# One expert slot loaded in pieces, products that nothing reads, and a first output store in two parts

## The reference

```python
def reference(x, p, ...):
    x = first_block(x, p, ...)      # stick-breaking and latent attention, conv + gated FFN, gated embedding
    x = second_block(x, c_2, ...)   # modulated conv / sparse attention / pooling mixer, then the experts
    return x

# the end of the second block
h = _rmsnorm(x, norm2_g) * (1 + sc2) + sh2
x = x + g2 * _hier_moe(h, ...)      # 32 experts in 4 groups; each token takes one group and its best two
return _rmsnorm(x, final_g)

# one expert, over the tokens that chose it
(silu(hb @ w1[e]) * (hb @ w3[e])) @ w2[e]      # 1024 -> 512 -> 1024
```

## Time and profile before

| | us |
|---|---|
| three runs, median (lowest to highest) | 928.71 (927.51 to 929.39) |
| the profiled execution, its own time | 927.32 |
| its span in the profile | 925.3 |
| PE busy / PEld / DVE / ACT / POOL | 780.2 / 528.0 / 382.2 / 327.5 / 125.7 |
| read from HBM | 296.55 MB |

### The profile page before, as it was taken

The page is one execution under the profiler, slowest core; times in us unless marked ns, Lnnn a source line. Parts: engine busy times, 40 slices in busy tenths (PEclk is TensorE's granted clock), DMA queues, the critical chain, the costliest instruction groups (busy, mean ns, idle before and its releaser), DMA issues.

```text
span 925.3 us, 12760 instructions
## 1 busy us (share of the span) xinstructions
PE 780.2 (84%) x5334; PEld 528.0 (57%) x5334; DVE 382.2 (41%) x837; ACT 327.5 (35%) x652; POOL 125.7 (14%) x129
## 2 busy tenths in 40 slices
PE   9999999999999999999999997567675566656765
PEld 7986578999998877898786342123221222212214
DVE  6747865667779764899613110010100101001002
ACT  5656656666665466834723010001000000000012
POOL 0011031555541034102110000000000000000000
PEclk9999999999999999999999999789878988988877
DMA  9956708754069782655479999999999999999995
GB/s 353 419 192 233 306 1 356 268 184 183 35 246 397 300 316 94 251 183 201 164 290 421 431 426 428 429 429 425 428 428 427 429 427 428 429 426 429 428 425 239
DMA packets 24543, 298.48 MB, mean 323 GB/s; under 512 B 2720, under 2 KB 3104, under 8 KB 5920
## 3 DMA queue, kind: packets, MB, share of 16 engines
q1 hardware_dynamic: 24480, 297.61, 78.3%
HBM read 296.55 MB, written 1.05 MB: 322 GB/s over the span
## 4 chain that ended last, share of the span: by engine, by line
PE 61%; DMA 33%; ACT 3%; DVE 2%; issue 0%; DVEq 0%; ACTq 0%
PE ps L108 60%; DMA ring<-in_exps 33%; PE ps L111 1%; ACT fr L117 1%; ACT sq L114 1%; ACT ar L117 0%; ACT ar L114 0%; DVE xg L134 0%; DVE ar L126 0%; DVE misc L149 0%; DVE yT L126 0%; ACT L114 0%; DVE yT L130 0%; DVE sq L134 0%; ACT hT L114 0%
## 5 line engine op out<-in xcount | busy, mean ns | idle before, releaser
L108 PE MATMUL ps<-fr 128*128 128x256 f32 (+2 forms) x1308 | 208.0, 316 | 0.9 <-POOL fr L126 0.4
L108 PE MATMUL ps<-ring,sq 128*32 128x512 f32 x944 | 137.4, 717 | 75.5 <-DMA ring<-in_exps 75.1
L108 PEld LDWEIGHTS ps<-fr 128*128 128x128 f32 (+1 forms) x1308 | 184.4, 191 | 18.5 <-DVE fr L126 1.9
L108 PE MATMUL ps<-ring,ar 128*32 128x512 f32 (+4 forms) x792 | 97.4, 583 | 45.5 <-DMA ring<-in_exps 39.4
L108 PEld LDWEIGHTS ps<-ring,sq 128*32 128x32 f32 x944 | 28.8, 121 | 172.6 <-DMA ring<-in_exps 119.7
L126 DVE TENSOR_TENSOR fr<-ring,fr 128x512 fp32r<-128x512 f32 (+2 forms) x121 | 93.8, 803 | 44.2 <-ACT fr L117 43.9
L126 DVE TENSOR_TENSOR ar<-ar,ps 128x512 f32<-128x512 f32 x9 | 6.2, 687 | 250.9 <-PE ps L108 250.9
L117 ACT ACTIVATE fr<-ring 128x512 fp32r<-128x512 f32 (+1 forms) x139 | 80.0, 622 | 25.9 <-PE ps L108 23.1
L117 ACT ACTIVATE ar<-ps 128x512 f32<-128x512 f32 (+4 forms) x48 | 27.2, 571 | 166.0 <-PE ps L111 139.4
L108 PEld LDWEIGHTS ps<-ring,ar 128*32 128x32 f32 (+1 forms) x792 | 26.6, 120 | 100.3 <-DMA ring<-in_exps 58.5
L126 DVE TENSOR_TENSOR ar<-ps,ar 128x512 f32<-128x512 f32 (+6 forms) x38 | 23.4, 632 | 117.2 <-PE ps L108 116.9
(11 more groups left out here) (187 smaller groups left out, 908.7 us busy)
## 6 DMA issues: line engine op xcount, KB each, us to landing
ring<-in_exps SPq DMA_DIRECT2D x85, 2048.0 KB, 30.9
ring<-in_modw SPq DMA_DIRECT2D x12, 2048.0 KB, 12.7
ring<-in_wup SPq DMA_DIRECT2D x11, 2048.0 KB, 13.3
ring<-in_wdown SPq DMA_DIRECT2D x5, 2048.0 KB, 12.8
ar<-in_exps SPq DMA_DIRECT2D x5, 2048.0 KB, 12.9
ring<-in_win SPq DMA_DIRECT2D x4, 2048.0 KB, 11.2
ring<-in_exps SPq DMA_DIRECT2D x7, 1024.0 KB, 9.0
ring<-in_wo SPq DMA_DIRECT2D x2, 2048.0 KB, 8.8
```

The lines of the kernel that those rows point to most:

```text
L108: return Issue(self.e and self.e.matmul(o, l, r, start=start, stop=stop, skip_group_check=True))
```

## The change

It does four things. Slot 8 is described as three pieces of 2048, 1536 and 512 columns; the third holds the place of the mask. The first two are issued after slot 5, with waits for the mask and for the last sum of the pooling, ahead of slot 7; the third follows slot 7. Slot 17, which has the same place, is loaded in the same three pieces. Slot 14 of the ring is loaded in halves like 12 and 13. PE gets products that nothing reads: 8 in the first joint, and in the last group 16 before each slot from the third on, 4 before the transposes, 3 after them and 12 between the first two parts of the end; PE's wait for a root of the first block (`act_wo["root", 1]`) is passed some instructions earlier. The first output tile is scaled and stored in two parts, each with 256 columns of either half.

```diff
--- before.py
+++ after.py
@@ -421,6 +421,7 @@
                  sd.rearrange("p a t -> p (a t)"), ar[:, 3584:4096]]
         more = {3: [hT[:, :], ar[:, 1536:3584]], 6: spare}
         more.update({7 + i: [ar[:, 4096 + SLOT * i:4096 + SLOT * (i + 1)]] for i in range(3)})
+        more[8] = [ar[:, 8192:10240], ar[:, 10752:12288], ar[:, 10240:10752]]
         more.update({17: more[8], 18: more[9]})
         part8, whole = misc[:, 16:32], misc[:, 32:38]
         END = GROUPS - 1
@@ -445,7 +446,7 @@
         def expert_in(j):
             if j in more:
                 return landed[f"again{j}" if j > 11 else f"more{j}"]["all"]
-            return loaded("exps", j, int(j in (12, 13)))
+            return loaded("exps", j, int(j in (12, 13, 14)))
 
 
         END_PARTS = ((0, 256), (256, 256), (512, 128), (640, 128), (768, 128), (896, 64), (960, 64))
@@ -764,8 +765,12 @@
 
             pe.wait_ge(act_wo["o", 1])
             to_features("mix", (6, 7, 0, 1))
+            pe.wait_ge(act_wo["root", 1])
+            idle_products(2, 5)
             token_sums("mix", 2, dve_joint["mix", "mt", 1, 0])
+            idle_products(3, 5)
             token_columns("mix", 2)
+            idle_products(3, 5)
             pe.wait_ge(dve_joint["mix", "rrecip"])
             turned_over(3, misc[:, 118:120]).then_inc(pe_joint, "mix", "over")
             mod_total(1, act_wo["root", 1])
@@ -1133,6 +1138,8 @@
                             over_tokens(j - 2)
                         for kk in range(2):
                             k = 2 * s + kk
+                            if g == END and 4 * m + s > 1 and kk == 0:
+                                idle_products(16, 2)
                             pe.wait_ge(expert_in(j))
                             if m == 0:
                                 pe.wait_ge(*x_ready(g, k))
@@ -1148,6 +1155,8 @@
                     spread_row(0, mod[:, 40:48], ((act_exp["x", 0, 7], dve_exp["x", 0, 6]), ()))
                 elif g < END:
                     gather(g + 1, 0)
+                if g == END:
+                    idle_products(4, 3)
                 pe.wait_ge(dve_exp["av", g])
                 for k in range(4):
                     t = pe.transpose(ps[:, 0, 128 * k:128 * k + 128], ar[:, av + 128 * k:av + 128 * k + 128], ident)
@@ -1179,6 +1188,7 @@
                     spread_row(1, col("final_g", 0, 8), ((dve_exp["x", 3, 3],), (act_exp["x", 3, 7],)))
 
 
+            idle_products(3, 3)
             pe.wait_ge(act_exp["aT", END], dve_exp["st", END])
             def end_sum(i):
                 lo, n = END_PARTS[i]
@@ -1202,6 +1212,7 @@
                 t.then_inc(pe_end, "y", i)
 
             end_products(0)
+            idle_products(12, 3)
             end_products(1)
             end_sum(0)
             end_sum(1)
@@ -1686,8 +1697,10 @@
                 row_root(whole[:, 2 + j:3 + j], whole[:, j:j + 1], 1024).then_inc(act_end, "root", j)
             for j in range(2):
                 act.wait_ge(dve_end["recip", j], dve_end["gain", 1])
-                o = sq[:, 1024 * j:1024 * j + 512]
-                act.copy(o, o, whole[:, 4 + j:5 + j]).then_inc(act_end, "out", j)
+                for i in range(2 - j):
+                    n = 512 if j else 256
+                    o = sq[:, 1024 * j + n * i:1024 * j + n * i + n]
+                    act.copy(o, o, whole[:, 4 + j:5 + j]).then_inc(act_end, "out", j, i)
 
         def vector(dve):
             def rest(signal, name, k, ready):
@@ -2271,9 +2284,11 @@
                 dve.wait_ge(act_end["root", j])
                 t = dve.reciprocal(whole[:, 4 + j:5 + j], whole[:, 2 + j:3 + j]).then_inc(dve_end, "recip", j)
                 dve.wait_ge(t)
-                o = 1024 * j + 512
-                dve.scalar_tensor_tensor(sq[:, o:o + 512], bank(YB[2 * j + 1]), whole[:, 4 + j:5 + j], ar[:, FROW + 512:FROW + 1024],
-                                         ALU.mult, ALU.mult).then_inc(dve_end, "out", j)
+                for i in range(2 - j):
+                    n = 512 if j else 256
+                    o = 512 + n * i
+                    dve.scalar_tensor_tensor(sq[:, 1024 * j + o:1024 * j + o + n], bank(YB[2 * j + 1], n * i, n * i + n), whole[:, 4 + j:5 + j],
+                                             ar[:, FROW + o:FROW + o + n], ALU.mult, ALU.mult).then_inc(dve_end, "out", j, i)
 
         def gpsimd(pool):
 
@@ -2421,7 +2436,7 @@
             def ring_load(name, j):
                 n = {("win", 3): 3584, ("wqkv", 0): 3072, ("wdown", 5): 2048, ("wple", 0): 2048, ("win2", 3): 2048,
                      ("wsm2", 0): 3104}.get((name, j), SLOT)
-                if name == "exps" and j in (12, 13):
+                if name == "exps" and j in (12, 13, 14):
                     for h in range(2):
                         sp.wait_ge(*used(*BEFORE[name, j], h))
                         sp.dma_start(slot(name, j)[:, 2048 * h:2048 * h + 2048],
@@ -2438,12 +2453,13 @@
                     return
                 sp.dma_start(slot(name, j)[:, 0:n], A[name][j][:, 0:n]).then_inc(ring_in[PLACE[name, j]], name, j, 0)
 
-            def more_load(j, name, *free):
+            def more_load(j, name, *free, places=(0, 8)):
                 lo = 0
                 sp.wait_ge(*free)
-                for o in more[j]:
+                for i, o in enumerate(more[j]):
                     n = o.shape[1]
-                    sp.dma_start(o, A["exps"][j][:, lo:lo + n]).then_inc(landed[name], "all")
+                    if places[0] <= i < places[1]:
+                        sp.dma_start(o, A["exps"][j][:, lo:lo + n]).then_inc(landed[name], "all")
                     lo += n
 
             for name, j in STREAM[:-2]:
@@ -2460,9 +2476,11 @@
                 if (name, j) == ("exps", 4):
                     more_load(3, "more3", pe_conv["qu", 1], dve_in2["glu"])
                 elif (name, j) == ("exps", 5):
+                    more_load(8, "more8", dve_in2["mask"], pool_conv["pm"], places=(0, 2))
                     more_load(7, "more7", pe_out2["pool", 1], pe_out2["rbias"], pe_soft["dsa", "values", 3], act_out2["at", 0], act_out2["at", 1],
                               dve_conv["tap", 30, 1], pool_conv["pm"], pool_conv["rwg"], dve_out2["rbias"], act_out2["pool", 1])
-                    for i in (8, 9, 6):
+                    more_load(8, "more8", places=(2, 3))
+                    for i in (9, 6):
                         more_load(i, f"more{i}")
                 elif (name, j) == ("exps", 16):
                     for i in (17, 18):
@@ -2475,9 +2493,12 @@
                     sp.wait_ge(*used(*BEFORE["exps", j]))
                 o, lo = last_place(i), lo % SLOT
                 sp.dma_start(ring[:, o:o + n], A["exps"][j][:, lo:lo + n]).then_inc(landed[f"last{i - 2}"], "all")
-            for j in range(2):
-                sp.wait_ge(act_end["out", j], dve_end["out", j])
-                sp.dma_start(out[:, 1024 * j:1024 * j + 1024], sq[:, 1024 * j:1024 * j + 1024]).then_inc(stored, "out", j)
+            for i in range(2):
+                sp.wait_ge(act_end["out", 0, i], dve_end["out", 0, i])
+                o, x = (v[:, 0:1024].rearrange("p (h c) -> p h c", c=512)[:, :, 256 * i:256 * i + 256] for v in (out, sq))
+                sp.dma_start(o, x).then_inc(stored, "out", 0, i)
+            sp.wait_ge(act_end["out", 1, 0], dve_end["out", 1, 0])
+            sp.dma_start(out[:, 1024:2048], sq[:, 1024:2048]).then_inc(stored, "out", 1)
 
 
         gT, grow, gbc, oa, osl, kept = 1024, 1536, 2048, 2560, 4608, 7936
@@ -2647,7 +2668,7 @@
             p = Program(e)
             sync(p)
             when_flagged(p, over_sync)
-            e.wait_ge(stored.sem, 32)
+            e.wait_ge(stored.sem, stored.final)
 
         @block.tensor
         def _(e):
```

## The result

The changed kernel takes 930.18 us (median of 20 runs, 928.78 to 933.83) against 928.47 for the kernel before in the same comparison (20 runs, 927.15 to 930.04). The ratio is 1.0021, with a 95% interval of 1.0013 to 1.0029: 1.9 us slower (1.2 to 2.7). The ratio is worked out from all runs and is not that of the two medians. The forecast was 927.5, no change or a little faster. So the two profiles lie 4.7 us apart, more than the medians do, and part of that is chance.

The account below looks back on a forecast made before the run. Up to 468 us compute was taken to set the time, from there the loads still to come. Terms -1.3 - 1.5 + 1.8 - 0.2 = -1.2 us gave a median of 927.5 us, range 924.9 to 930.0.

Parts of the forecast that it names:

- A: First joint: eight products keep the clock up, so the FFN's 24 matmuls take 3.06 instead of 4.43 us; -1.3 us.
- the "yes" to whether the next weight tile is ready: FFN's start: the tile is ready at 150.1 us, before PE gets to it at 150.3 after 48 matmuls.
- B: Slot 8 in early pieces: 4.30 us leave the stream behind 468, a restart at slot 12 takes part back; -1.5 us.
- 1.65 us earlier than now, and all behind it by the same: Slot 12's first half lands at 502.35 us, 1.65 earlier, and all later loads keep that gain.
- The load of 468.0: 2 MB load that met an empty queue: 8.0 us to landing instead of 4.91, pricing a restart at 3.1 us.
- Rival 3: One upstream gain missing: slot 12's half still needs 7.2 us, or the joint's clock falls anyway; 929.0 us, chance 0.16.
- C: Last group: sixteen products make a slot cost PE 5.64 us while one lands every 4.91; +1.8 us.
- Rival 4: Last group's products run at the low clock, making the change slower: 931.0 us, chance 0.08.
- D: First output tile's store in parts: first store up to 0.4 us earlier, last up to 0.4 later; -0.2 us.
- The rivals with a gain (1 and 2): First: last group's products never delay PE, 925.7 us, chance 0.22; second: slot 12's restart costs less, 926.2 us, chance 0.10.

Follow-up runs that it names:

- the group alone: Kernel before with only the idle products of the last group added: 930.36 us, ratio 1.0024 (1.0014 to 1.0035).
- The parts alone: Kernel before with one part each: joint products and earlier wait, 0.9984; slots 8, 14, 17 in pieces or halves, 0.9995; last group's products, 1.0024.

## Why the prediction was wrong

- **A, -1.3, was right in size**: -1.5 measured (0.6 to 2.4), the joint 0.12 longer where 0.1 was taken, 24 matmuls in 3.10 where 3.06 was worked out. One step in it failed, the "yes" to whether the next weight tile is ready: PE waits for it and some 0.3 us are lost, 1.0 instead of 1.3 against the profile of before. That the measured gain is no smaller than forecast is luck: the other executions without the products mostly lose more than that profile (5.0 to 5.3 us for the 24 matmuls in three of five, 4.6 in one). That the kernel before loses this time in most executions, but not in all, one profile could not show.
- **B, -1.5, was wrong**, in the step "1.65 us earlier than now, and all behind it by the same". The first clause held: 5.1 us from issue to landing (5.55 forecast), 1.86 us earlier. By the Trainium skill, DMA: Bandwidth & Descriptors, section Anatomy of one DMA, it would have been 4.4 us, an estimate from what that page gives for loads issued by GpSimd; the 5.1 of this trace, for a load issued by SP, does not bear it out. The second clause failed at once. A restart was priced once, for one half; but slot 12's second half is also issued only when PE lets its place go, 2.1 us after the first. It meets a queue as thin and pays again: 4.30 us behind the first half instead of 2.45, which puts it where it was. The load of 468.0, from which the price was taken, did not show this: its successor stood in the queue 0.4 us later and landed 5.3 us behind it, near the 4.91 of the full stream. Rival 3 had B's gain missing (sum +0.3), but for slot 12's first half, the one that did gain.
- **C, +1.8, was too small.** The mechanism held in every number that the profile of before could give: 5.62 us a slot (5.64), 0.73 lost with each, no idle time, full clock; alone it cost 2.2 us (1.3 to 3.3), in the changed kernel 3.5. What was missed is how PE enters the group. The earlier trace rows begin with a group entered at full clock; in nine of the fourteen profiles the slot before it runs at the low clock and takes 2.9 to 3.6 us instead of 1.9. PE then comes to the third slot 1.8 us later against its landing (2.54 late in the changed kernel, 0.76 with the group alone), and as it has no idle time from there on, all of that reaches the end: 4.9 us of lag there against 2.4 (a late landing in the latter is the other 0.6). Without the products 2.8 us of idle time before the third slot absorb it. Whether the low clock there is chance or comes with the other parts stays open: eight of the nine profiles whose FFN starts at full clock have it, and one of the five others. Rival 4 looked for the low clock inside the group, where it never came.
- **D, -0.2**: nothing in the traces, and below what the runs can tell.
- **The sum**: the forecast's -1.2 lies 3.1 below the measured +1.9. With C as the changed kernel has it (3.5) it missed B by 1.5 and C by 1.7. That -1.5 and 0 and 3.5 and 0 come to the measured value proves little, since the 3.5 is itself the measured value less the rest. The parts alone (-1.5, -0.5 and +2.2) come to 0.2. The late entry into the last group would make up for that, but each term is known to about 1 us, so that C grows beside the other parts is argued from the profiles and not shown by the times. The rivals with a gain (1 and 2) were wrong in C's size or in B's, and the range, which ended at 930.0, missed the median by 0.2 us. Its upper end took in one missing gain (929.0), but not a missing gain and a larger C together.

## What to carry to other kernels

Work put in to keep TensorE's clock up is free only while it fits into the wait that it fills: measure the period of the stream, and stay below it with a margin for a late entry (4.73 us against 4.9 here, not 5.62). Loading something earlier gained next to nothing here, because loads behind it wait for places that the compute sets free: look for the last load that a release issues into a thin queue, and count only the bytes behind it.

## What was not expected of the hardware

- With few loads queued the DMA engines look busy but move less: 0.96 busy at 339 GB/s and 0.93 at 334 between 498 and 507 us, against 1.01 and 427 in a full stream. Why the packets take longer there stays open.
- The start of the program varies by up to 1.3 us between executions with nothing changed: the first matmuls are issued every 0.427 us until some moment between 4.0 and 7.4 us, then every 0.216. The Trainium skill, TensorE: Matmul & The Clock Gate, section on the HAM clock gate, says that the gate does not begin anew with a kernel, so that the number of slow matmuls differs from run to run. The traces agree in the number, 5 to 13 spacings of 0.427 us in the fourteen profiles; that the clock is the cause they do not show, as it is not recorded there. The FFN's start without the joint's products differs from one execution to the next as well, and perhaps the slot ahead of the last group does. One profile of a kernel shows one draw of it.
